# Moving small startup loads behind the first projections, taking two mixed row sets in turn, and placing constant products in TensorE's first gaps

## The reference, cut to what matters

```python
mod = cs @ p['ada_w'][l] + p['ada_b'][l]
h = modulate(rmsnorm(x, p['norm_g'][l, 0]), sh1, sc1)

shifted = jnp.concatenate([prev_x[:, None, :].astype(h.dtype), h[:, :-1]], axis=1)
xm = h[:, :, None, :] + (shifted - h)[:, :, None, :] * p['rw_mu'][l].astype(h.dtype)   # six mixed sets
rkv = jnp.einsum('bsnd,nde->bsne', xm[:, :, :3], p['rw_w_rkv'][l])
xw, xa, xg = xm[:, :, 3], xm[:, :, 4], xm[:, :, 5]
w_log = -jax.nn.softplus(-(p['rw_w0'][l] + jnp.tanh(xw @ p['rw_w1'][l]) @ p['rw_w2'][l])) - 0.5
a = jax.nn.sigmoid(p['rw_a0'][l] + (xa @ p['rw_a1'][l]) @ p['rw_a2'][l])
g = jax.nn.sigmoid(xg @ p['rw_g1'][l]) @ p['rw_g2'][l]
kk = heads(k * p['rw_k_k'][l])
```

## Time and profile before

| | us |
|---|---|
| median of 3 runs | 1238.1 (1236.4 to 1241.33) |
| the profiled execution, its own time | 1236.46 |
| its span, first to last instruction | 1234.7 |
| PE busy (matmuls) | 1108.7 (90%) |
| DVE busy | 539.8 (44%) |
| ACT busy | 340.7 (28%) |
| POOL busy | 56.4 (5%) |
| mean granted TensorE clock | 0.968 of full |

### The profile page before, as it was taken

One profiled execution on the slowest core, in us unless ns is written; L12 is line 12 of the kernel. 1 busy time (PEld: TensorE's weight loads), 2 busy tenths in 40 slices (PEclk: granted clock), 3 DMA queues, 4 the chain that ended last, 5 costly groups with the idle time before them and its releaser, 6 DMA issues.

```text
span 1234.7 us, 22208 instructions
## 1 busy us (share of the span) xinstructions
PE 1108.7 (90%) x8949; PEld 637.3 (52%) x8949; DVE 539.8 (44%) x1419; ACT 340.7 (28%) x650; POOL 56.4 (5%) x66
## 2 busy tenths in 40 slices
PE   5479998999887989999999988998999999999984
PEld 2136666788873546344444445565766344444443
DVE  3430357668224163344444445133464344444443
ACT  2112231222230031433333231233331333333222
POOL 2000000000000000000000000000000010000000
PEclk9689999999997999999999999999999999999997
DMA  9631312651328750699999964557430499999931
GB/s 233 217 136 69 136 69 76 231 195 61 140 104 345 301 239 1 283 416 426 426 426 424 424 225 155 216 185 275 166 127 1 182 416 428 425 426 427 421 132 43
DMA packets 45971, 297.11 MB, mean 241 GB/s; under 512 B 5956, under 2 KB 7336, under 8 KB 22344
## 3 DMA queue, kind: packets, MB, share of 16 engines
q1 hardware_dynamic: 43856, 290.17, 58.9%
q0 software_dynamic: 1840, 5.79, 2.0%
q10 hardware_dynamic: 200, 0.06, 0.0%
HBM read 293.77 MB, written 2.24 MB: 240 GB/s over the span
## 4 chain that ended last, share of the span: by engine, by line
PE 80%; DVE 10%; DMA 5%; ACT 2%; issue 2%; SPq 0%; ACTq 0%; DVEq 0%; POOL 0%; POOLq 0%
PE bank L728 78%; DMA ring<-in_ada_w 4%; DVE work L1627 2%; ACT work L1360 2%; DVE work L1633 1%; DVE ring L1627 1%; DVE rstd L1665 1%; DVE x_res L2012 1%; DMA ring<-in_rw_w_rkv 1%; DVE work L1630 1%; PE bank L1142 1%; DVE work L1998 1%; DVE work L1739 0%; PE bank L1346 0%; DMA work<-in_kv_ada_w 0%
## 5 line engine op out<-in xcount | busy, mean ns | idle before, releaser
L728 PE MATMUL bank<-ring,work 128*64 128x512 f32 (+1 forms) x1600 | 341.2, 579 | 9.3 <-DVE work L1998 7.6
L728 PE MATMUL bank<-work,ring 128*128 128x320 f32 (+3 forms) x1600 | 300.1, 362 | 25.5 <-DVE work L1633 6.8
L728 PEld LDWEIGHTS bank<-work,ring 128*128 128x128 f32 (+2 forms) x1600 | 208.5, 168 | 117.5 <-issue 32.9
L728 PE MATMUL bank<-work 128*128 128x320 bf16 (+7 forms) x1906 | 222.2, 279 | 22.9 <-DVE x_res L2012 7.7
L728 PEld LDWEIGHTS bank<-ring,work 128*64 128x64 f32 (+1 forms) x1600 | 112.9, 137 | 210.7 <-issue 203.6
L728 PEld LDWEIGHTS bank<-work 128*128 128x128 bf16 (+3 forms) x1906 | 163.1, 122 | 91.5 <-issue 23.8
L1360 ACT ACTIVATE work<-bank 128x320 f32<-128x320 f32 (+6 forms) x115 | 57.7, 543 | 242.2 <-PE bank L728 212.1
L1992 DVE SCALAR_TENSOR_TENSOR work<-work,small,bank 128x256 f32<-128x256 f32 x32 | 21.5, 673 | 168.7 <-ACT work L1532 89.2
L2012 DVE SCALAR_TENSOR_TENSOR x_res<-bank,mod,x_res 128x256 f32<-128x256 f32 (+1 forms) x256 | 86.2, 378 | 18.4 <-PE bank L728 4.6
L728 PE MATMUL bank<-ring 64*64 64x64 f32 (+2 forms) x1984 | 78.1, 227 | 1.9 <-issue 1.0
L728 PEld LDWEIGHTS bank<-ring 64*64 64x64 f32 (+2 forms) x1984 | 69.1, 136 | 15.3 <-issue 12.1
(11 more groups left out here) (191 smaller groups left out, 808.3 us busy)
## 6 DMA issues: line engine op xcount, KB each, us to landing
ring<-in_moe_w_gu SPq DMA_DIRECT2D x64, 2048.0 KB, 13.9
ring<-in_moe_w_down SPq DMA_DIRECT2D x64, 1024.0 KB, 14.3
ring<-in_ada_w SPq DMA_DIRECT2D x32, 1024.0 KB, 5.2
ring<-in_rw_w_rkv SPq DMA_DIRECT2D x6, 2048.0 KB, 7.8
ring<-in_ada_w SPq DMA_DIRECT2D x4, 2048.0 KB, 29.1
work<-in_kv_ada_w SPq DMA_DIRECT2D x8, 1024.0 KB, 5.6
work<-in_ada_w SPq DMA_DIRECT2D x8, 1024.0 KB, 8.5
ring<-in_rw_w_o SPq DMA_DIRECT2D x2, 2048.0 KB, 11.2
```

The lines of the kernel that those rows point to most:

```text
L728: return eng.matmul(out, l, r, start=start, stop=stop, **kw)
```

## The change

It has four parts, all in the order and place of work that exists or of constant work.

1. POOL's loads of `const_wkv` stand behind the shift row's two puts. The four router loads and the two sink loads stand behind a new wait for "kk raw", the first product of VectorE after the projections with `rw_w_rkv` 1.
2. The bank that collects the `mod` rows is held out of the turn. Three `keep_busy` products follow each of the first three `ada_w` sets, and one follows the last, ahead of the turn.
3. Five `keep_busy` products follow the turn, and five more follow the shift row's transposes.
4. VectorE makes mixed sets 3 and 4 in turn, chunk by chunk, where it made all eight chunks of set 3 ahead of those of set 4. The other four sets stay as they are.

```diff
-            eng.dma_start(cph[:, 0:WN], i["const_wkv"]).then_inc(in_sems["wkvc_in"], 16)
-            for h in range(2):
-                eng.dma_start(sink[64 * h:64 * h + 64, :],
-                              i["at_sinks"][0].rearrange("(c h) -> h c", h=2)[h:h + 1, :].broadcast_to([64, C]),
-                              allow_slow_non_contiguous=True).then_inc(in_sems["sink_in"], 16)
...
-            for l in range(2):
-                load_router(l)
...
             pl.wait("shift row")
             put(o[2][0, 0].rearrange("(c p) -> c p", p=P), shiftT[0:C, 0:P])
             put(o[6][0, 0].rearrange("(c p) -> c p", p=P), shiftT[0:C, P:2 * P])
+            eng.dma_start(cph[:, 0:WN], i["const_wkv"]).then_inc(in_sems["wkvc_in"], 16)
+            pl.wait("kk raw")
+            for l in range(2):
+                load_router(l)
+            for h in range(2):
+                eng.dma_start(sink[64 * h:64 * h + 64, :],
+                              i["at_sinks"][0].rearrange("(c h) -> h c", h=2)[h:h + 1, :].broadcast_to([64, C]),
+                              allow_slow_non_contiguous=True).then_inc(in_sems["sink_in"], 16)
...
-            pb = bank.open("mod", -1)
+            pb = bank.hold("mod", -1)
             for m in range(4):
                 s = arrived(pe, "ada", m)
                 for c in range(2):
                     ins = mod_rows(pb, 2 * m + c, slot(s, 4096)[:, 2048 * c:2048 * c + 2048])
                 pe.did(ins, ("used", "ada", m), ("mod", -1))
+                if m < 3:
+                    keep_busy(3)
+            bank.held.clear()
+            keep_busy(1)
             mod_turn(-1)
-
+            keep_busy(5)
...
             full(ins, "shift")
+            keep_busy(5)
...
+            for c in range(C):
+                for n in MIX[0:2]:
+                    stt(xm[n][:, c, :], diff[:, c, :], vcol("rw_mu", 8 * n + c), h0[:, c, :], M, A_, ("xm", n, c),
+                        ("xm", n))
             for k, n in enumerate(MIX):
-                if k >= 2:
-                    ve.wait("xm used", MIX[k - 2])
+                if k < 2:
+                    continue
+                ve.wait("xm used", MIX[k - 2])
```

## The result

The changed kernel takes 1232.2 us (median of five runs, 1228.9 to 1233.0) against 1238.1. The ratio is 0.9944, with an interval of 0.9922 to 0.9966: a gain of about 7 us, between 4 and 10 (the two medians alone differ by 5.9). The forecast was 12.5 us (1225.6). The median lies 0.7 us above the top of the range; the ratio, which uses all runs, puts the changed kernel at 1231.2 and thus just inside it. The direction was right, and the forecast gain was nearly twice the measured one. The profiled execution took 1231.73 (span 1229.9), only 4.7 us less than that of before.

A forecast was written before the change was run, and what follows sets the result against it. The startup was taken as one serial path, with `ada_w` delayed by GpSimd's small loads. Terms of -8.4 and -3.3 gave -11.7 us: 1224.8 from the profile, 1226.4 from the median, stated as 1225.6, range 1219.5 to 1231.5.

The forecast's parts named there:

- What bounds the kernel: First 180 us: one serial path, `ada_w` late because GpSimd's small sink and router loads held the DMA engines at 12-21 us.
- Part 1: Startup loads: with GpSimd's loads moved, the four `ada_w` loads land at about 18, 23, 28 and 34 us or sooner.
- Part 2: adaLN stretch: nine constant products put 5.1 us on the path; VectorE's mod step at 39.7, 8.4 us earlier.
- Parts 3 and 4: After the turn: both groups of five products hidden at full clock; mixed sets 3 and 4 in turn worth 3.3 us.
- Part 5: GpSimd's moved loads: `const_wkv` lands before its reader; routers and sinks cost others 0 to 5 us, nearest 0.
- The sum's last step: Behind the third mixed set, all follows at its old distances, so the whole -11.7 us reaches the end.
- T2: Theory formed after the measurement, not forecast: lead is lost in later stages because constant products shift the turn of the banks.
- A: Rival: clock lost once in the startup, slowing the second group of five or g products; about 1229, chance 0.16.
- E: Rival: more gain, as first inputs gain 1.6 us and turn and shift their tenths; about 1222.5, chance 0.10.
- B: Rival: adaLN weight isn't earlier, slow stretch has another cause or shifts onto `ada_w`; -4.9 us, about 1232, chance 0.06.
- C: Rival: moved loads collide with the third projection's weights; 5 to 8 us given back, about 1231, chance 0.05.
- D: Rival: sets and constant products run at half clock after the mean square; +9.7 us, about 1246, chance 0.03.

The follow-up runs named there:

- x1: Kernel before with only the loads moved (`const_wkv`, routers, sinks), no constant products, mixed sets in old order: 1225.9 us, ratio 0.9888.
- x7: Changed kernel without the ten constant products among the adaLN sets; the two groups of five stay: 1225.7 us, ratio 0.9884.
- x6: Kernel before with the loads moved and mixed sets 3 and 4 in turn, no constant products: 1222.4 us, ratio 0.9873.
- x10: Kernel before with the constant products alone, loads and mixed sets as they were: 1241.4 us (12 runs), ratio 1.0014.
- x2: Kernel before with only mixed sets 3 and 4 made in turn: 1234.5 us, ratio 0.9961.
- x11: Kernel before with loads moved, sets in turn, no constant products, and low-rank weights in ring slot 1 in place of 0: 1211.4 us, ratio 0.9795.
- x12: Kernel before with ten constant products ahead of the recurrence as a pure delay: 1246.8 us, ratio 1.0058.
- x8: Changed kernel without the ten products among the sets, and low-rank weights in ring slot 1 in place of 0: 1215.8 us, ratio 0.9805.
- x5: Changed kernel with two more bank openings (no work) behind the last constant products, restoring the old turn of banks: 1230.9 us, ratio 0.9929.
- x9: Changed kernel timed again with no edit, beside the kernel before: 1230.4 us, ratio 0.9940.

## Why the prediction came out as it did

**What bounds the kernel.** Right for the first 200 us. The small elements in GpSimd's queue were the cause of the slow stretch: with them gone the same 9 us carry 3.80 MB in place of 0.70. I had blamed sinks and routers together; the trace after puts the stretch down to the two sink loads, 4 KB in all.

**Part 1.** Right. The last load was seen at 31.71 in x1, a little ahead of my 34 (or sooner). The first inputs gained nothing to be seen: 10.96, 10.65 and 11.85 in the three traces of after, 10.58 and 11.67 in the two of before.

**Part 2.** The sizes were right, and the 0.1 us at the mod step are partly luck, as it stood at 38.71 and 40.53 in the other two traces. The 5.1 us on the path are real: x7 has its mod step at 34.89 and its recurrence at 195.44, 4.7 and 5.0 us ahead of the means of the three traces of the changed kernel, and x6 is better than the changed kernel in the ratio by 0.0067 to 0.0071, with intervals that don't meet. I had written that the first three groups would stand on the path and still took the change as it is for the better by the whole sum; that holds against before, but of the 8 to 9 us by which x6 is better than the changed kernel, 5.9 are already there at the recurrence.

**Parts 3 and 4.** Both groups of five were hidden as worked out, and the alternation was worth 3.3 in the sum (the subtraction written there gives 3.2) and 3.1 at the third set between x1 and x6 (52.77 and 49.63). That the second group is of no use once VectorE paces PE I hadn't drawn from my own line, which said that the pairs keep pace at either clock.

**Part 5.** Right. `const_wkv` landed 4.2 us after its issue, and the slow stretch of the sinks at 128 to 137 made nobody wait. It met no large load, so what it costs one wasn't tested there.

**The sum's last step failed: that the lead at 83 us arrives at the end one for one.** The sum took everything behind the first wait for projection weights as a fixed length. For a pure shift the step holds as far as the intervals tell, and for the loads, the alternation and both as well. It fails for the changed kernel and for x10. The lead is the start of the recurrence in the kernel's own trace against 211.05, the mean of the two traces of before; the gain is the ratio times the median of before beside it. "Shifted by" says by how many of the eight banks the turn is displaced behind the startup:

| kernel | products in the startup | shifted by | lead, us | gain, us (interval) | lost, us |
|---|---|---|---|---|---|
| x1 | 0 | 0 | 13.1 | 13.9 (10.8 to 17.0) | -0.8 |
| x2 | 0 | 0 | 3.6 | 4.8 (2.6 to 7.2) | -1.2 |
| x6 | 0 | 0 | 16.6 | 15.8 (11.9 to 19.5) | 0.8 |
| x11 | 0 | 0 | 25.0 | 25.4 (22.3 to 28.6) | -0.4 |
| x12 | 0 | 0 (1 from the recurrence on) | -8.6 | -7.2 (-9.9 to -4.3) | -1.4 |
| x8 | 10 | 2 | 23.8 | 24.2 (20.2 to 28.2) | -0.4 |
| x7 | 10 | 2 | 15.6 | 14.4 (10.7 to 18.1) | 1.2 |
| x5 | 20 | 0 | 9.4 | 8.8 (5.7 to 11.9) | 0.6 |
| changed kernel, x9 | 20 | 6 | 9.6 | 7.4 (4.7 to 10.2) | 2.2 |
| changed kernel, first | 20 | 6 | 10.6 | 6.9 (4.2 to 9.7) | 3.7 |
| x10 | 20 | 6 | 2.7 | -1.7 (-4.3 to 1.0) | 4.5 |

The lead lies outside the interval of the gain in the last two rows, and in x9 too if the mean of the changed kernel's three traces (10.7) is taken. There 2 to 5 us are missing: this is the term that the sum put at nothing. In x5, x7 and x8, which have constant products too, nothing is lost that the intervals can tell. **Its cause stays open.** Twenty constant products go with it, and so does a turn of the banks shifted by six: x5, which has the twenty and the old turn, lost 0.6. So T2 is not excluded, nor shown, as the intervals of x5 and of the changed kernel overlap. A kernel with the shifted turn and no products would tell, and wasn't run. The loss may lie behind the recurrence, or ahead of it in executions that weren't traced: the lead comes from one trace, and the traced execution of x10 was its fastest. What can be said is that in most kernels the time of a run follows its mean granted clock, and that products which raise the clock early bought nothing when they were added alone.

Part of the miss is a matter of the base. The profiled execution of before had a rest of 1023.0, where a median of 1238.7, less 211.05 and the 1.8 us around the span, leaves 1025.9, so the profiled pair shows 4.7 us where the timings show 7.

**The rivals.** A (the clock lost once in the startup) is excluded by the granted clock of 1.00 in 47 to 54 us and the third mixed set at 54.78, E (more than the sum) by the first input at 10.96. B (the weight isn't earlier) is excluded by the 422 GB/s, C (the moved loads collide) by PE's two waits, D (half clock among the sets) by the rows of 1.92 us, each in the traces at hand. The time of about 1232 that came was B's, but not by B's mechanism. None of my rivals was a loss far behind the change.

## What to carry to other kernels

Ask first which transfer stands behind the first long wait, and look at the queues' shares of engine time, not at bytes: a queue that moved 0.05 MB held up 8 MB, most likely by two loads of 2 KB. Constant products that keep TensorE's clock stay off the path only while something else holds the engine up (and even there they gained nothing in x10); the edit that removes the wait puts them on the path, and where VectorE paces the products no clock is needed. Before a gain is taken from one trace, see how much the same program varies behind the change (here 6.5 us), and look for the next wait on the same chain: moving one load to another slot was worth more than the constant products cost.

## What the runs showed of the hardware that wasn't expected

A wait of 3.1 us ahead of the same 24 MATMULs was followed by 6.70 us in one execution of the kernel before and by 9.76 in another. So the granted clock behind such a short idle stretch isn't a property of the program. The Trainium skill, TensorE: Matmul & The Clock Gate, What's actually happening, says that the point of transition varies from run to run; these rows agree.

Two loads of 2 KB each (`at_sinks`, elements of 4 bytes) took 9.6 us to land and over half of all 16 engines' time for 10 us, where the router loads of 128 KB issued just ahead of them landed in 3.1.

`const_wkv`, 640 KB on GpSimd's queue, landed 4.2 us after its issue while VectorE ran its two-input instructions without a gap, against 9.8 when it shared the engines with the startup. No delay by VectorE's work showed.
